# A two-layer hybrid decoder step: sample sums between the row tiles, and one transpose turn behind the next projection

## What is computed

```python
def rmsnorm(x, g):
    y = x * rsqrt(mean(x * x, axis=-1) + EPS)
    return y * g
# attention: three groups (window, dilation) = (128, 1), (512, 4), (2048, 16), 16 heads of 64 channels
s = einsum('bqhd,bkhd->bhqk', q, k) * ATTN_SCALE    # masked by the band
p = exp(s - max(s)); l = sum(p)
o = einsum('bhqk,bkhd->bqhd', p, v) / l             # the groups are then combined by a softmax of their denominators
# experts
out = out + (silu(gate) * up * combine) @ w_down    # for each expert; x = x + out
y_prompt, y_sample = rmsnorm(x_prompt, norm_final), rmsnorm(x_sample, norm_final)
```

## Time and profile before

| | us |
|---|---|
| median of 3 runs | 1703.19 (1701.74 to 1704.39) |
| the profiled execution | 1704.07 |
| its span | 1702.3 |
| PE busy | 1641.2 (96%) |
| DVE busy | 634.2 (37%) |
| ACT busy | 451.8 (27%) |

### The profile page before, as it was taken

The page is one execution under the profiler, slowest core; times in us unless marked ns, Lnnn a source line. Parts: engine busy times, 40 slices in busy tenths (PEclk is TensorE's granted clock), DMA queues, the critical chain, the costliest instruction groups (busy, mean ns, idle before and its releaser), DMA issues.

```text
span 1702.3 us, 21530 instructions
## 1 busy us (share of the span) xinstructions
PE 1641.2 (96%) x8123; PEld 956.1 (56%) x8123; DVE 634.2 (37%) x1374; ACT 451.8 (27%) x1167; POOL 137.6 (8%) x280
## 2 busy tenths in 40 slices
PE   7999999999999999999999999989999999999997
PEld 5877777643444344435878878756644443444342
DVE  3689983422222222214033354654422222222123
ACT  3477761211111111112152242232311111111111
POOL 1223330100000000002001002310000000000000
PEclk9999999999999999999999999999999999999999
DMA  9557676499999999997436618776399999999994
GB/s 343 188 178 220 196 233 249 157 399 427 427 429 427 428 429 427 428 425 289 155 113 225 253 63 318 193 223 265 154 371 410 426 428 428 428 428 428 427 428 176
DMA packets 101382, 538.02 MB, mean 316 GB/s; under 512 B 7964, under 2 KB 32740, under 8 KB 76690
## 3 DMA queue, kind: packets, MB, share of 16 engines
q1 hardware_dynamic: 85622, 485.20, 70.3%
q0 software_dynamic: 15360, 51.30, 9.7%
q10 hardware_dynamic: 316, 0.37, 0.1%
HBM read 520.61 MB, written 16.42 MB: 315 GB/s over the span
## 4 chain that ended last, share of the span: by engine, by line
PE 77%; DVE 8%; ACT 7%; DMA 6%; issue 2%; POOL 0%; DVEq 0%; SPq 0%; ACTq 0%; POOLq 0%
PE bank L942 25%; PE bank L954 12%; PE bank L1302 8%; PE bank L928 6%; PE bank L814 4%; PE bank L1199 4%; PE bank L948 4%; PE bank L1227 3%; DMA ring<-in_moe_w_gate_up 3%; PE bank L1149 3%; DMA arena<-sample_queries 2%; PE bank L1493 2%; DVE arena L2109 2%; ACT arena L1825 2%; DVE arena L2343 1%
## 5 line engine op out<-in xcount | busy, mean ns | idle before, releaser
L942 PE MATMUL bank<-ring,arena 128*64 128x512 f32 x1536 | 339.4, 597 | 8.1 <-DMA ring<-in_moe_w_gate_up 5.4
L1302 PE MATMUL bank<-hT,ring 128*128 128x264 f32 x1152 | 271.7, 392 | 0.0
L1302 PEld LDWEIGHTS bank<-hT,ring 128*128 128x128 f32 x1152 | 217.0, 192 | 44.3 <-issue 9.1
L942 PEld LDWEIGHTS bank<-ring,arena 128*64 128x64 f32 x1536 | 113.5, 138 | 226.6 <-issue 225.5
L2109 DVE TENSOR_TENSOR arena<-arena,bank 128x512 f32<-128x512 f32 x32 | 34.3, 1071 | 389.3 <-ACT arena L1607 389.3
L954 PE MATMUL bank<-ring,arena 128*64 128x512 f32 x768 | 170.1, 595 | 0.9 <-ACT arena L1609 0.9
L948 PE MATMUL bank<-arena 128*128 128x512 f32 x256 | 126.9, 618 | 1.7 <-ACT arena L1617 1.6
L1607 ACT ACTIVATE arena<-bank 128x512 f32<-128x512 f32 x32 | 19.1, 597 | 400.1 <-PE bank L942 400.1
L814 PE MATMUL bank<-ident,arena 128*128 128x128 f32 (+5 forms) x609 | 100.8, 279 | 23.5 <-DVE arena L1901 10.5
L2056 DVE SCALAR_TENSOR_TENSOR arena<-arena 128x1024 f32<-128x1024 f32 x32 | 41.1, 1285 | 217.0 <-ACT arena L1617 217.0
L814 PEld LDWEIGHTS bank<-ident,arena 128*128 128x128 f32 (+5 forms) x609 | 70.6, 141 | 82.4 <-issue 37.8
(11 more groups left out here) (328 smaller groups left out, 1726.8 us busy)
## 6 DMA issues: line engine op xcount, KB each, us to landing
ring<-in_moe_w_gate_up SPq DMA_DIRECT2D x96, 2048.0 KB, 18.1
ring<-in_moe_w_down SPq DMA_DIRECT2D x48, 2048.0 KB, 22.6
arena<-in_moe_w_gate_up SPq DMA_DIRECT2D x32, 2048.0 KB, 17.6
ring<-in_attn_qkv SPq DMA_DIRECT2D x18, 2048.0 KB, 9.1
arena<-in_moe_w_down SPq DMA_DIRECT2D x16, 2048.0 KB, 22.1
ring<-in_ssm_in_proj SPq DMA_DIRECT2D x10, 2048.0 KB, 13.7
out<-arena POOLq DMA_DIRECT2D x24, 512.0 KB, 4.0
arena<-in_cache_kv_w POOLq DMA_DIRECT2D x20, 512.0 KB, 7.6
```

The source lines that it names most:

```text
L942: mm = pe.matmul(bank[j][e * SLOTS:(e + 1) * SLOTS, :], Xg[:, 4 * half + k, 2 * (p % 2) + e, :], weights(2 * half + e, p)[:, k, j * DE:(j ...
L1302: mm = pe.matmul(bank[i % 2][:, 0:T], wv[:, k, (i % 4) * P:(i % 4 + 1) * P], hT[:, k, :], start=(k == 0), stop=(k == DT - 1))
```

## The change

**First**, at the end of both expert stages, the samples' two products (PE) and sums (DVE) go between the sums of row tile 0 and those of row tile 1. In norm 2 and norm 4 the order of squares, variances, roots and stores becomes row tile 0, samples, row tile 1 (`NORM_ORDER`); norm 0 keeps its order. As the squares of the samples are now written before the last scatters have read their operands, the area `xn_a` moves to the start of the arena. **Second**, in groups 0 and 1 of the attention `turn(g, 0, 1)` goes where group 2 has it, behind `qkv_tile` of step 2.

```diff
-        xn_a = Area(3 * D + DT * T)(3, D)
+        xn_a = Area(0)(3, D)
+        NORM_ORDER = {0: (0, 1, 2), 2: (0, 2, 1), 4: (0, 2, 1)}
@@ SP, end: the stores follow NORM_ORDER[4]
-            for t in range(2):
-                sp.wait_ge(n_xn, XN_BASE[4] + t + 1)
-                sp.dma_start(y_p[0, t * P:(t + 1) * P], X[:, t, :]).then_inc(s_out, 16)
-            sp.wait_ge(n_xn, XN_BASE[4] + 3)
-            sp.dma_start(y_s.rearrange("b s d -> (b s) d"), X[0:NS, 2, :]).then_inc(s_out, 16)
+            for i, t in enumerate(NORM_ORDER[4]):
+                sp.wait_ge(n_xn, XN_BASE[4] + i + 1)
+                if t < 2:
+                    sp.dma_start(y_p[0, t * P:(t + 1) * P], X[:, t, :]).then_inc(s_out, 16)
+                else:
+                    sp.dma_start(y_s.rearrange("b s d -> (b s) d"), X[0:NS, 2, :]).then_inc(s_out, 16)
@@ PE, end of the experts
-                for j in range(4):
-                    if j >= 2:
-                        pe.wait_ge(s_xa, 12 * l + 6 + j - 1)
+                for j in range(2):
                     scatter(j)
                 pe.wait_ge(s.ys, more * PAIRS + PAIRS + 2)
                 for q in range(2):
                     pe.matmul(bank[q][0:NS, :], selT[:, :], acc_s[:, q, :], start=True, stop=True).then_inc(s_ot, 1)
+                for j in range(2, 4):
+                    pe.wait_ge(s_xa, 12 * l + 6 + j - 1)
+                    scatter(j)
@@ PE, lagging and the loop over the steps
-                if 1 <= s <= DT and (g < NGRP - 1 or s > 1):
+                if 1 < s <= DT:
                     turn(g, s - 1, 1)
@@
-                    if g == NGRP - 1 and t == 2:
+                    if t == 2:
                         turn(g, 0, 1)
@@ ACT, norm
-                squares(0, P)
-                squares(1, P)
-                root(0, P)
-                squares(2, NS)
-                root(1, P)
-                root(2, NS)
+                t0, t1, t2 = ((t, ROWS[t]) for t in NORM_ORDER[k])
+                squares(*t0)
+                squares(*t1)
+                root(*t0)
+                squares(*t2)
+                root(*t1)
+                root(*t2)
@@ DVE, norm 2 (norm 0 keeps the old order)
+                    variance(k, 2, NS)
+                    link(row_scale(0, P))
+                    rows(0)
+                    variance(k, 1, P)
+                    row_scale(2, NS).then_inc(n_var, 1)
+                    link(row_scale(1, P))
+                    rows(1)
@@ DVE, end of the experts
-                add(last, s_xa)
-                variance(k + 1, 0, P)
+                add(last, s_xa, range(2))
                 for q in range(2):
                     v.wait_ge(s_ot, 8 + 8 * l + q - 1)
                     xs = X[0:NS, 2, 512 * q:512 * q + 512]
                     v.tensor_tensor(xs, xs, bank[q][0:NS, :], ALU.add).then_inc(s_xa, 1)
+                variance(k + 1, 0, P)
+                add(last, s_xa, range(2, 4))
@@ DVE, norm 4
-            variance(4, 1, P)
-            for t, r in enumerate(ROWS):
-                v.wait_ge(n_std, VAR_BASE[4] + t + 1)
+            variance(4, 2, NS)
+            v.wait_ge(s_vld, 128)
+            for i, t in enumerate(NORM_ORDER[4]):
+                r = ROWS[t]
+                if i == 1:
+                    variance(4, 1, P)
+                v.wait_ge(n_std, VAR_BASE[4] + i + 1)
```

More of the change, by code:

```diff
@@ L1524, in squares @@
                     if k:
-                        act.wait_ge(s_xa, 6 * (k - 1) + 2 * (t + 1))
+                        act.wait_ge(s_xa, 6 * (k - 1) + 2 * (NORM_ORDER[k].index(t) + 1))
                     act.activation(xn[0:r, t, :], X[0:r, t, :], ACT.Square, accum_out=ss[0:r, t:t + 1]).then_inc(n_ss, 1)
                 def root(t, r):
-                    act.wait_ge(n_var, VAR_BASE[k] + t + 1)
+                    act.wait_ge(n_var, VAR_BASE[k] + NORM_ORDER[k].index(t) + 1)
                     act.activation(rstd[0:r, t:t + 1], ss[0:r, t:t + 1], ACT.Sqrt).then_inc(n_std, 1)
@@ L1890, in variance @@
             def variance(k, t, r):
-                v.wait_ge(n_ss, SS_BASE[k] + t + 1)
+                v.wait_ge(n_ss, SS_BASE[k] + NORM_ORDER[k].index(t) + 1)
                 v.tensor_scalar(ss[0:r, t:t + 1], ss[0:r, t:t + 1], 1.0 / D, EPS, ALU.mult, ALU.add).then_inc(n_var, 1)
@@ L1896, in row_scale @@
                 def row_scale(t, r):
-                    v.wait_ge(n_std, VAR_BASE[k] + t + 1)
+                    v.wait_ge(n_std, VAR_BASE[k] + NORM_ORDER[k].index(t) + 1)
                     return v.reciprocal(rstd[0:r, t:t + 1], rstd[0:r, t:t + 1])
@@ L1901, in rows @@
                     v.tensor_scalar(xn[:, t, :], X[:, t, :], rstd[:, t:t + 1], None, ALU.mult).then_inc(n_xn, 1)
[L1903 to L1909, removed]
+                if k == 0:
+                    variance(k, 1, P)
[5 more added lines that the diff above has]
+                    rows(1)
+                else:
+                    variance(k, 2, NS)
+                    link(row_scale(0, P))
+                    rows(0)
+                    variance(k, 1, P)
+                    row_scale(2, NS).then_inc(n_var, 1)
+                    link(row_scale(1, P))
+                    rows(1)
                 if k == 0:
@@ L2044, in tokens, with add @@
                                         [P, 2, 4, FREE]), ALU.mult).then_inc(s.xg, 1)
-                def add(n, done):
-                    for j in range(4):
+                def add(n, done, js=range(4)):
+                    for j in js:
                         v.wait_ge(s.sc, n * 4 + j + 1)
@@ L2467, in _ @@
             moe(1)
-            variance(4, 1, P)
-            for t, r in enumerate(ROWS):
-                v.wait_ge(n_std, VAR_BASE[4] + t + 1)
+            variance(4, 2, NS)
[5 more added lines that the diff above has]
+                v.wait_ge(n_std, VAR_BASE[4] + i + 1)
                 link(v.reciprocal(rstd[0:r, t:t + 1], rstd[0:r, t:t + 1]))
-                if t == 0:
-                    variance(4, 2, NS)
-                    v.wait_ge(s_vld, 128)
                 v.scalar_tensor_tensor(out=X[0:r, t, :], in0=X[0:r, t, :], scalar=rstd[0:r, t:t + 1],
```

## The result

The changed kernel takes 1708.69 us in the median of 8 runs (1705.16 to 1713.45), the kernel before 1701.38 in 8 runs beside it (1696.31 to 1704.39). The ratio is 1.0038 with an interval of 1.0025 to 1.0050: slower by 4 to 9 us. The eight runs of the kernel before include the three that stood ahead of the prediction (median 1703.19). The profiled execution took 1709.63 us, its span is 1707.9 us.

What follows compares the result with a forecast made beforehand. PE was taken to bound the kernel, in the head loop held by DVE's mask and ACT's exponents and copies. 2.65 + 1.89 - 0.40 - 0.20 = +3.94 us, +7.34 with clock; on 1703.2: 1710.5 us, range 1706.0 to 1713.5.

Steps and rivals of the forecast that it cites:

- the clock holds in one place: Rival: PE's clock stays up behind one or both new waits, +3.9 to +5.6 us, 1707.1 to 1708.8; chance 0.24.
- Part 1: Head loop, groups 0 and 1: the moved turn delays DVE's mask, so PE waits longer: +2.65 and +1.89 us.
- the order pays as it reads: Rival: DVE masks the third tile as scores land, PE's old waits vanish, norms gain too: -3.1 us, 1700.1; chance 0.10.
- L2343 of the third tile: Sign: whether DVE's mask of the third tile starts before or after the moved turn; 0.5 us behind it meant right.
- Part 2: Head loop, groups 0 and 1: PE's clock falls behind each new long wait, 1.7 us each, 3.4 in sum.
- stays low longer: Rival: the clock stays low longer because the 0.7 us wait and the long one add up: 1711.5 to 1714; chance 0.11.
- Part 3: Experts' end and norm 2: samples' sums between the row tiles gain 0.40 us (0.3 to 0.6).
- The end: Norm 4 and last stores: products end earlier but a larger store leaves last; gain 0.2 us, bounds -1.0 and +0.3.
- What could absorb it: Whether experts' DMA waits or group 2's cached key jobs give lost time back: they move along, nothing counted.

Runs made afterwards that it cites:

- e3: Kernel before with the turn moved in groups 0 and 1 and a third masked-score buffer there; norms as before: 1702.72 us, ratio 0.9999.
- e5: e2 with 12 (group 0) and 13 (group 1) products that nobody reads in PE's long wait: 1707.76 us, ratio 1.0025 against the kernel before.
- e2: Kernel before with the turn alone moved in groups 0 and 1, sums and norms as before: 1710.15 us, ratio 1.0048.
- e6: Kernel before with the turn moved in group 0 only: 1708.70 us, ratio 1.0047.
- e7: Kernel before with the turn moved in group 1 only: 1705.75 us, ratio 1.0021.
- e9: Whole change plus third masked-score buffer and ACT's copy of the moved turn behind the third tile's exponents, groups 0 and 1: 1699.00 us, 0.9979 against kernel before.
- e13: The kernel of e9 run once more: 1699.07 us, ratio 0.9982 against the kernel before.

## Why the prediction was right

It said 1710.5 us (1706.0 to 1713.5); 1708.69 was measured, against 1701.38 for the kernel before, whose first three runs, known to the forecast, had a median of 1703.19. By the difference, +7.3 was said and +7.3 is between the medians, +6.5 by the ratio. That the medians agree to the tenth is luck: beside the experiments the kernel before had medians of 1702.27 to 1703.52. The time alone doesn't choose between the forecast and the rival *the clock holds in one place* (+3.9 to +5.6), since the interval begins at +4.3; the traces do.

**Part 1** held in mechanism and size. The mask starts 0.53 us behind the moved turn (0.56 was taken); waits of 0.67 and 2.98 us stand where 0.74 and 2.85 were written, in group 1 0.67 and 3.23 for 0.74 and 3.26; sums +2.63 and +1.86 for +2.65 and +1.89. What carried it was one line of code, the wait of `masked` on `h_t`, and e3 shows that it is this line: with a free buffer the loss is gone. The rival *the order pays as it reads* is refuted for the kernel as changed. Its own condition, a mask ahead of the moved turn, is met in e3, and even there it doesn't pay as it was priced (-3.1): the second follower, ACT's copy ahead of the exponents, was not in its price, nor was what group 2 takes back. The prediction gave "L2343 of the third tile" as the only deciding point, and that was one too few.

**Part 2** held in mechanism: both waits are followed by a fall, and filling them (e5) takes it away. Its size, 1.7 us each from the earlier trace rows, is that of four of the six falls traced: 6.56 - 4.97 = 1.59 and 1.63 in e2, 1.63 in e6, 1.64 in e7. Over many runs e2 less e5 gives 2.4 us (medians) to 3.9 (ratios) for both, where 3.4 was said. But the profiled execution of the change has 3.06 and 2.91, because the clock stays low for 6.8 us, as in the rival *stays low longer*, priced at 1711.5 and more. That it took 1709.63 all the same is partly luck: other falls that the kernel before had in its profile, among them one behind norm 2, are shorter or missing. Why the clock stays low for 3.4 us in one kernel and 6.8 in the other isn't known.

**Part 3**, norm 2: -0.49 for -0.40, but by two errors that cancel. The last sum was to end 785.93 - 779.77 = 6.16 us behind the first scatter, and it ends 6.44 behind: two scatters take 1.91 us of PE (781.32 to 783.23), not 2 x 0.86, as the four of the earlier trace rows could have told (783.73 - 779.77 = 3.96). On the other hand the chain behind it was called "the same in kind". It is 0.37 us shorter, mostly since its last step is DVE's scaling of row tile 1 (0.86 us) and not ACT's of the samples (1.15).

**The end**: -0.38 from the tail's first scatter for -0.20, a little more than the 0.3 that bounded the gain. The first product begins 0.16 us behind the last sum; the third ends 4.26 behind it, where 1699.0 less a last sum at 1694.3 made 4.7. The larger last store costs 0.87 us more between its issue and the end, and takes back most of it. The Trainium skill ("DMA: Bandwidth & Descriptors", "Anatomy of one DMA") puts a fixed cost of some 2 us, with the bytes on top, to a DMA issued by GpSimd. These stores are issued by SP, and it fits both within 0.3 us: 2.17 us for 32 KB (an estimate of 2.1), and 3.04 for 512 KB, where 2 us and the bytes at 400 to 430 GB/s make an estimate of 3.2 to 3.3.

**What could absorb it**: nothing was counted, and nearly nothing did. From the five transposes of group 0 to those of group 1 it is 119.10 us, 5.51 more than before (982.51 - 863.41 less 977.63 - 864.04), for 2.63 of waits and 3.06 of clock: 0.2 came back. The wait at group 2's start (0.75 for 0.61) gave nothing back.

## What to carry to other kernels

An instruction that is moved to let its engine run on takes along everything that waits for it: here a buffer that DVE wanted back, and a copy that stood ahead of other work in ACT's order. Search the code for every wait on its semaphore before moving it; with the buffer alone untied the two stretches gained 0.23 us together, with both 0.92, and neither showed in the time as long as the norms stayed as before. A new wait of 3 us on PE cost half as much again in clock in four of six cases and about as much again in two, and products that nobody reads, put into it, take that part away but not the wait.

## What was not expected of the hardware

- The falls of the clock don't sit at fixed places. The wait of 2.17 us in group 2 is followed by 6.8 us at 0.50 in the kernel before and by no fall in e9; one fall behind norm 2 comes in the trace of e13 and not in that of e9, which is the same kernel. Single profiles of this kernel therefore differ by several us in stretches that no edit touched, and its runs spread over 8 us.
- Behind nearly the same wait (2.98 us in the kernel after and in e2) the clock stayed low for 6.8 us in one and 3.4 in the other.
- The wait of group 2's first scores, for DVE's work on the cached keys, varies from 0 to 3.41 us, with no edit near it.
